# Further expert rows of a mixture-of-experts decoder layer: plain float32 products in four column tiles, bounded row gathers

## The reference

```python
A = T * TOP_K                                   # 1024 * 8 routed rows
counts = jnp.bincount(e_flat, length=N_EXPERTS)
...
def body(acc, blk):
    rows, rw, e = blk                           # a block of rows of one expert, with their weights
    xb = x_pad[rows]
    h = jax.nn.silu(xb @ w_gate[e]) * (xb @ w_up[e])    # 1024 -> 256, twice
    yb = (h @ w_down[e]) * rw[:, None]                  # 256 -> 1024
    return acc.at[rows].add(yb), None
```

## Time and profile before

| what | value |
|---|---|
| median of 3 runs | 1641.52 us (1641.01 to 1644.18) |
| the profiled execution, own time | 1632.95 us |
| its span, first to last instruction | 1631.3 us, mean granted TensorE clock 0.979 |
| PE busy | 1574.2 us (97%) |
| DVE, ACT, POOL busy | 1183.2, 1033.3, 505.7 us |
| moved by DMA | 368.63 MB |
| chain that ended last | PE 78%, DVE 7%, issue 4%, ACT 3%, DMA 3% |

### The profile page before, as it was taken

One profiled execution on the slowest core, in us unless ns is written; L12 is line 12 of the kernel. 1 busy time (PEld: TensorE's weight loads), 2 busy tenths in 40 slices (PEclk: granted clock), 3 DMA queues, 4 the chain that ended last, 5 costly groups with the idle time before them and its releaser, 6 DMA issues.

```text
span 1631.3 us, 32225 instructions
## 1 busy us (share of the span) xinstructions
PE 1574.2 (97%) x8262; PEld 1310.3 (80%) x8263; DVE 1183.2 (73%) x2038; ACT 1033.3 (63%) x1709; POOL 505.7 (31%) x495
## 2 busy tenths in 40 slices
PE   6999999999999999899999999999999999999987
PEld 6997888888887788788888888788888888888864
DVE  4215777777777788838777888767876787888856
ACT  3215666666666645427667877766776777877855
POOL 0000000000000135532544454543554455454426
PEclk9999999999999999899999999999999999999995
DMA  7223222212223524568999999999998999999987
GB/s 247 91 82 96 67 59 65 71 45 71 58 65 111 185 108 170 196 218 315 318 303 309 304 363 360 329 289 263 331 322 276 286 356 326 348 365 370 366 252 283
DMA packets 161319, 368.63 MB, mean 226 GB/s; under 512 B 53008, under 2 KB 73488, under 8 KB 161264
## 3 DMA queue, kind: packets, MB, share of 16 engines
q1 hardware_dynamic: 136272, 284.21, 49.9%
q0 software_dynamic: 24992, 83.73, 19.8%
HBM read 294.39 MB, written 65.11 MB: 220 GB/s over the span
## 4 chain that ended last, share of the span: by engine, by line
PE 78%; DVE 7%; issue 4%; ACT 3%; DMA 3%; ACTq 2%; POOL 1%; SPq 0%; DVEq 0%; POOLq 0%
PE bank_pair L1032 6%; PE bank_pair L1035 6%; PE bank_pair L1038 6%; PE q_ps L91 4%; PE out_ps L923 4%; PE q_ps L93 4%; PE q_ps L92 4%; PE k_ps L901 4%; PE out_ps L1091 4%; PE out_ps L1092 3%; PE q_ps L1022 3%; PE k_ps L1059 3%; PE k_ps L1060 2%; PE k_ps L1067 2%; DVE gu_lo L1926 2%
## 5 line engine op out<-in xcount | busy, mean ns | idle before, releaser
L1926 DVE TENSOR_TENSOR gu_lo<-raw_gu,gu_hi 128x1024 fp32r<-128x1024 f32 x260 | 306.4, 1219 | 28.7 <-ACT gu_hi L1404 28.7
L1404 ACT CAST gu_hi<-raw_gu 128x1024 fp32r<-128x1024 f32 x260 | 253.3, 1050 | 6.0 <-DMA raw_gu<-in_moe_w_up_dram 6.0
L1032 PE MATMUL bank_pair<-gu_hi,xb_hi 128*128 128x512 f32 x576 | 235.5, 409 | 5.4 <-DVE gu_lo L1926 4.2
L1035 PE MATMUL bank_pair<-gu_lo,xb_hi 128*128 128x512 f32 x576 | 229.1, 398 | 0.0
L689 POOL DMA_INDIRECT sums_scratch<-ys,sidx x63 | 119.8, 1902 | 151.7 <-DMA sums_scratch<-ys,sidx 110.6
L1926 DVE TENSOR_TENSOR dn_lo<-raw_dn,dn_hi 128x1024 fp32r<-128x1024 f32 x130 | 152.6, 1213 | 2.2 <-ACT dn_hi L1404 1.7
L1038 PE MATMUL bank_pair<-gu_hi,xb_lo 128*128 128x512 f32 x576 | 142.7, 390 | 0.0
L1032 PEld LDWEIGHTS bank_pair<-gu_hi,xb_hi 128*128 128x128 f32 x576 | 111.5, 194 | 29.5 <-issue 6.5
L1309 ACT CAST pt_hi<-k_ps 128x512 fp32r<-128x512 f32 (+1 forms) x192 | 85.9, 482 | 74.2 <-PE k_ps L901 73.4
L620 POOL IOTA e<- 128x64 f32 x1 | 0.2, 185 | 426.6 <-DVE xs L1722 426.6
L1404 ACT CAST dn_hi<-raw_dn 128x1024 fp32r<-128x1024 f32 x130 | 130.0, 1051 | 3.2 <-DMA raw_dn<-in_moe_w_down_dram 3.2
(11 more groups left out here) (306 smaller groups left out, 3971.5 us busy)
## 6 DMA issues: line engine op xcount, KB each, us to landing
raw_gu<-in_moe_w_gate_dram SPq DMA_DIRECT2D x128, 512.0 KB, 6.6
raw_gu<-in_moe_w_up_dram SPq DMA_DIRECT2D x128, 512.0 KB, 9.1
raw_dn<-in_moe_w_down_dram SPq DMA_DIRECT2D x128, 512.0 KB, 8.9
wqk<-in_fox_w_in_dram SPq DMA_DIRECT2D x66, 128.0 KB, 2.4
v_scratch<-v_out SPq DMA_DIRECT2D x32, 256.0 KB, 2.8
va<-v_scratch SPq DMA_DIRECT2D x16, 512.0 KB, 4.7
fin<-sums_scratch SPq DMA_DIRECT2D x16, 512.0 KB, 9.0
xs<-in_x_dram SPq DMA_DIRECT2D x8, 512.0 KB, 7.8
```

The lines of the kernel that those rows point to most:

```text
L1032: i = pe.matmul(o3, xb_hi[s][:, c], g_hi[:, :, c], start=c == 0, stop=False, skip_group_check=True)
L1035: pe.matmul(o3, xb_hi[s][:, c], g_lo[:, :, c], start=False, stop=False, skip_group_check=True)
L1404: a.copy(hi, raw).then_inc(S[done], 1)
L1926: dve.tensor_tensor(lo, raw, hi, ALU.subtract).then_inc(S[lo_ok], 1)
```

## The change

Further rows no longer use split operands. `xo` and `ho` hold the 32 rows as plain float32, and PE multiplies them by the raw weights. The 32 stationary columns take a quarter of PE's columns, so four products stand side by side: result rows 0 to 31, 32 to 63, 64 to 95 and 96 to 127 of the PSUM bank are four column tiles. For gate and up they are gate and up of an even chunk, and gate and up of an odd chunk; 16 matmuls of 256 columns. For down they are two chunks by two halves; 4 matmuls of 512 columns. ACT and DVE add the partial results in two pieces where there was one, and two DVE steps that made lo parts go.

Since the raw weights are now read until the further rows are done, `raw_gu` gets a third buffer (sets go to places 0, 2, 1 in turn), and the loads wait for PE: gate and up of set s for the start of `gate_up` of expert s - 3 (`started`), down of set s for the end of `down` of expert s - 3 (`downed`). Room for the third buffer comes from smaller and shared tiles: `tab` becomes 16-bit and is converted by POOL once, `gu_x` and the further results lie in free partitions of `x_rows2`. Six experts stand in a loop now, and two more before it.

The four indirect DMAs over rows get a bound of T - 1 and skip what lies above: padded slots are neither gathered nor added.

The diff, cut to its core:

```diff
-            raw_gu = [sb(f"raw_gu{i}", [P, 2, DC, FF], c=m) for i in range(2)]
+            raw_gu = [[sb(f"raw_{n}{i}", [P, DC, FF], c=m) for n in ("gate", "up")] for i in range(2)]
...
-            xo = sb("xo", [P, DC, P], F32R, c=m)
-            ho = sb("ho", [P, FC, P], F32R, c=m)
-            gu_x = sb("gu_x", [XR, 2 * FF], c=m)
-            ys = [sb(f"ys{i}", [P, D], c=m) for i in range(3)]
-            sg = sb("sg", [P, FF], c=m)
-            hh = sb("hh", [P, FF], c=m)
+            xo = sb("xo", [P, DC, XR], c=m)
+            ho = sb("ho", [P, FC, XR], c=m)
+            gu_x = xg[2][2 * XR:3 * XR, 0:2 * FF]
+            ys_x = xg[2][3 * XR:P, 0:D]
+            y_half = xg[2][2 * XR:P, BANK:D]
+            ys = [sb(f"ys{i}", [P, D], c=m) for i in range(2)]
...
+            raw_gu.append([third_gate, sb("raw_up2", [P, DC, FF], c=m)])
+            tab_in = raw_gu[2][1][:].rearrange("p c f -> p (c f)")[:, 0:TAB].bitcast(I32)
...
+        def raw_place(s):
+            return s if s < 2 else (0, 2, 1)[(s - 2) % 3]
+        def g_piece(s, k):
+            c = slice((k % 2) * 4, (k % 2) * 4 + 4)
+            return (raw_gu[raw_place(s)][k // 2][:, c], split[s % 2][0][:, k // 2, c], split[s % 2][1][:, k // 2, c])
...
+        ROUND = 6
+        ROUNDS = (E - 4) // ROUND
...
+            def next_gate_up(s, place):
+                if place > 3:
+                    sp.wait_ge(S["started"], SH + s - 2)
+                    stand(sp)
+                load_gate_up(place, *(w[ds(s - 1, 1)].rearrange("o k n -> (o k) n") for w in (w_gate, w_up)),
...
+            def next_down(s, place):
+                if place > 2:
+                    sp.wait_ge(S["downed"], SH + s - 2)
+                    stand(sp)
+                load_down(place % 2, w_down[ds(s - 1, 1)].rearrange("o k n -> (o k) n"),
...
-            next_gate_up(3, 1)
-            with sp.Fori(0, E // 2 - 2) as i:
-                for par in range(2):
-                    next_gate_up(2 * i + (par + 4), par)
-                    next_down(2 * i + (par + 3), 1 - par)
-            next_gate_up(E, 0)
-            next_down(E - 1, 1)
-            next_down(E, 0)
+            sp.dma_start(tab_in, tab_dram.rearrange("(p n) o -> p (n o)", p=P)).then_inc(S["c_loads"], 16)
+            sp.wait_ge(S["c_const"], 11)
+            next_gate_up(3, 3)
+            with sp.Fori(0, ROUNDS) as i:
+                for u in range(ROUND):
+                    next_gate_up(ROUND * i + (u + 4), u + 4)
+                    next_down(ROUND * i + (u + 3), u + 3)
+            next_gate_up(E, E)
+            next_down(E - 1, E - 1)
+            next_down(E, E)
...
-                                     in_offset=bass.IndirectOffsetOnAxis(ap=gidx[i][:, 0:1], axis=0)).then_inc(got[i], 16)
+                                     in_offset=bass.IndirectOffsetOnAxis(ap=gidx[i][:, 0:1], axis=0),
+                                     bounds_check=T - 1, oob_is_err=False).then_inc(got[i], 16)
...
-                                     in_=ys[par][:], in_offset=None, compute_op=ALU.add).then_inc(sent[par], 16)
+                                     in_=ys[par][:], in_offset=None, bounds_check=T - 1, oob_is_err=False, compute_op=ALU.add).then_inc(sent[par], 16)
...
-                    pool.wait_ge(S["c_loads"], 64)
+                    if b + 2 == SH:
+                        pool.wait_ge(S["c_loads"], 64)
+                        g.tensor_copy(tab[:], tab_in).then_inc(S["c_const"], 1)
+                        g.memset(xg[2][0:2 * XR], 0.0).then_inc(S["c_const"], 1)
+                        for i in range(2):
+                            g.memset(xg[i][:, D:ROW_W], 0.0).then_inc(S["c_const"], 1)
+                        pool.wait_ge(S["c_const"], 14)
...
-            def gate_up_further(w, x):
-                g_hi, g_lo = split[w][0:2]
-                o3 = out_ps[:, BANK:T].rearrange("p (g f) -> p g f", g=2)
-                pe.wait_ge(S["x_rows_lo_ok"], x + 1)
+            def gate_up_further(s, x):
+                raw = raw_gu[raw_place(s)]
+                pe.wait_ge(S["x_rows_ok"], x + 1)
                 pe.wait_ge(S["x_scaled"], x + 1)
-                for c in range(DC):
-                    pe.matmul(o3, xo[:, c], g_hi[:, :, c], start=c == 0, stop=False, skip_group_check=True)
-                    i = pe.matmul(o3, xo[:, c], g_lo[:, :, c], start=False, stop=c == DC - 1, skip_group_check=True)
+                for c in range(0, DC, 2):
+                    for j in range(4):
+                        i = pe.matmul(out_ps[x_tile(j), BANK:BANK + FF], xo[:, c + j // 2], raw[j % 2][:, c + j // 2], start=c == 0,
+                                      stop=c == DC - 2, skip_group_check=True)
...
-            def down_further(w, nset, x):
-                d_hi, d_lo = split[w][2:4]
-                pe.wait_ge(S["x_ht_lo_ok"], x + 1)
-                pe.wait_ge(S["d_lo_ok"], D_PIECES * nset)
-                for r in HALVES:
-                    for c in range(FC):
-                        pe.matmul(out_ps[:, r], ho[:, c], d_hi[:, c, r], start=c == 0, stop=False, skip_group_check=True)
-                        i = pe.matmul(out_ps[:, r], ho[:, c], d_lo[:, c, r], start=False, stop=c == FC - 1, skip_group_check=True)
+            def down_further(e, s, x, by_rows=True):
+                raw = raw_dn[s % 2]
+                pe.wait_ge(S["x_ht_ok"], x + 1)
+                pe.wait_ge(d_raw[s % 2], 8 * D_PIECES * (e + 1 - s % 2) + 16 * D_PIECES)
+                stand(pe)
+                for j in range(4):
+                    c, half = (j // 2, j % 2) if by_rows else (j % 2, j // 2)
+                    i = pe.matmul(out_ps[x_tile(j), BANK:T], ho[:, c], raw[:, c, HALVES[half]], start=True, stop=True, skip_group_check=True)
...
-            with pe.Fori(0, E // 2 - 1) as i:
-                for par in range(2):
-                    expert(2 * i + par, par)
-            expert(E - 2, 0)
-            expert(E - 1, 1, last=True)
+            for e in range(2):
+                expert(e, e)
+            with pe.Fori(0, ROUNDS) as i:
+                for u in range(2, ROUND + 2):
+                    expert(ROUND * i + u, u)
...
-                a.copy(gu_x[:], out_ps[XR:2 * XR, BANK:T]).then_inc(S["x_half"], 1)
+                a.copy(gu_x[:, 0:FF], out_ps[x_tile(2), BANK:BANK + FF]).then_inc(S["x_half"], 1)
+                a.copy(gu_x[:, FF:2 * FF], out_ps[x_tile(3), BANK:BANK + FF]).then_inc(S["x_up_half"], 1)
...
-                dve.tensor_tensor(gu_x[:], out_ps[0:XR, BANK:T], gu_x[:], ALU.add).then_inc(S["x_sum"], 1)
+                dve.tensor_tensor(gu_x[:, 0:FF], out_ps[x_tile(0), BANK:BANK + FF], gu_x[:, 0:FF], ALU.add).then_inc(S["x_sum"], 1)
+                dve.wait_ge(S["x_up_half"], x + 1)
+                dve.tensor_tensor(gu_x[:, FF:2 * FF], out_ps[x_tile(1), BANK:BANK + FF], gu_x[:, FF:2 * FF], ALU.add).then_inc(S["x_up_sum"], 1)
...
-                dve.tensor_tensor(ys[2][0:XR], out_ps[0:XR, :], ys[2][0:XR], ALU.add).then_inc(S["x_scaled"], 1)
+                dve.tensor_tensor(ys_x[:, BANK:D], out_ps[x_tile(1), BANK:T], ys_x[:, BANK:D], ALU.add)
+                dve.tensor_tensor(ys_x[:, 0:BANK], out_ps[x_tile(0), BANK:T], y_half[0:XR], ALU.add).then_inc(S["x_scaled"], 1)
...
```

More of the change, by code:

```diff
@@ L492, in _, with load_gate_up @@
                 weights_out(t - 1)
-            def load_gate_up(par, gate, up, left):
+            def load_gate_up(place, gate, up, left):
                 for k in range(G_PIECES):
@@ L1170, in _, with expert @@
                     logits(TT - 1)
-            def expert(e, par, last=False):
+            def expert(e, u, last=False):
+                par = u % 2
                 w = 1 - par
```

181 lines of the change are left out of this document (95 added, 86 removed).

## The result

The changed kernel takes 1780.41 us (median of 4 runs, 1774.61 to 1785.89), 1.0841 times the kernel before (95% interval 1.0794 to 1.0889). The forecast was 1581 us, and its range ended at 1618. It is slower by 139 us where 61 us less were forecast.

What follows compares the result with a forecast made beforehand. PE was taken to bound the expert stage, transfers 10% behind. PE's 726 us, 755 with partly lost smoothing, plus 11 of waits gave 766 against 827: 61 us off 1641.5, about 1581 us; range 1556 to 1618.

Steps and rivals of the forecast that it cites:

- rival (c): Six-expert loop's code no longer stays; each of ten returns waits for a fetch, 23 to 92 us, 23 taken: 1604; chance 0.15.
- PE's own time: Expert stage: each further block costs PE 2.6 us less, 78 us over 30 blocks, leaving 726 us of pure PE.
- A full drain at each of four edges: Changing PE's tiling mode might drain the engine: 1.6 us per further block, 47 us in all; 0.36 per block taken instead.
- I cost them at nothing: DVE's and ACT's changed steps stay hidden behind gate_up; without that cover, 24 us either way.
- The late loads: Later requests lose part of the smoothing between short and long bodies: stage 755 us instead of 726, plus 11 of earlier waits.
- (a): Transfers take over fully in the expert stage, no smoothing left: saving 47, with more late-load waits 40, about 1598; chance 0.18.
- (b): Skipped padded rows still take a descriptor's slot, so no transfer time is saved: floor 11.7 us per body, 1590; chance 0.08.
- Rival (d): Loads come too late for every body in the expert stage, none under 14.0 us: 55 us more, 1697; chance 0.06.
- Rival (e): Column tiles of the further products do not run side by side: 5.1 us more per block, 153 us, 1795; chance 0.02.
- Full smoothing: Best case for the expert stage: long bodies cover all transfer waits of short ones, so it takes PE's 726 us.
- the edges at nothing: Entering and leaving PE's column tiling costs nothing, instead of 0.36 us per further block; used for the range's lower end.
- The tail and POOL's start: Last expert's block in the tail gains nothing; POOL's conversion and fills, 7 us before the first gather, stay hidden.

Runs made afterwards that it cites:

- a_short: Changed kernel with loops of two experts on SP, PE, ACT and DVE; further products read fixed weights of expert 0, except the last expert's: 1627.3 us, 0.9943.
- a_lean: Changed kernel, still six experts per loop, one copy of each part and no inner loops for more than one further block: 1610.8 us, 0.9804 of the kernel before.
- s_early: a_lean_late with the load times of the kernel before, loops of two experts and fixed weights for further products: 1573.0 us, 0.9567 of the kernel before.
- a_lean_late: a_lean with PE reading its three counts after the gate and up product, not at the body's start: 1598.7 us, 0.9736 of the kernel before.
- b_va6: Kernel before with only DVE's and ACT's expert loops six experts long, PE's left at two: 1694.1 us, 1.0347.
- b_pe4: Kernel before with only PE's expert loop made four experts long: 1640.3 us, 0.9982.
- b_late: Kernel before with only the changed kernel's two waits in SP's queue, so loads are asked for later: 1666.5 us, 1.0126.
- a_compact: Changed kernel, still six experts per loop, with one copy of a body's first half and of the down product: 1691.6 us, 1.0336 of the kernel before.
- b_pe6: Kernel before with only PE's expert loop made six experts long: 1709.6 us, 1.0441.
- a_gen: Changed kernel with six experts per loop, one copy of each part, counts read late, more than one further block kept compactly: 1599.9 us, 0.9722 of the kernel before.
- ll_nobound: a_lean_late without the bounds on the four indirect transfers, so padded slots are gathered and added: 1598.0 us, 0.9720 of the kernel before.

## Why the prediction was wrong

**Where the 139 us are**, by differences of the ratios times 1641.8 us. The lines add up by construction, as each starts from the kernel at which the one before it ends, so the sum is no check. Only the third line is a single edit. The second, the fourth and the last also change the length of the loops and whether the further products read fixed weights; a_short and a_lean differ by 16 us in the shortest bodies, of the fourth line's 23:

| step | us |
|---|---|
| further products, counts covered, loads as before (s_early) | -71 |
| loads asked for later (a_lean_late against s_early) | +28 |
| counts in the open (a_lean against a_lean_late) | +11 |
| two copies and the inner loops in the code (a_short against a_lean) | +23 |
| code that does not stay (changed against a_short) | +147 |
| sum | +138 |

**The step that failed is rival (c), the loop code: its price, and then its chance.** I had the mechanism and the rule of the Trainium skill that spoke for it (Runtime: NRT & Kernel Launch, Instruction fetch mechanics), gave it 0.15, and left its cost out of the sum. I priced it as one fetch per return, 2.3 to 9.2 us, and took 23 us in all. The runs show 147 us, some 14.7 us of waits per round. PE alone fetches ten to twelve packets per round, not one; DVE and ACT fetch theirs; PE waits for them as well as for itself (57 us in b_va6), and in other bodies of the round than the one at the return. After the long wait at 1266.29 the clock costs too (0.63 us per matmul, above). The sum had no term for this: even the upper end of my own price, 92 us, is too low. That before's loops showed no fetch, told nothing of a longer one, as I wrote; b_pe4, with no loss at four experts, shows how little it told. What I had was the rule, and I went against it.

**PE's own time was nearly right.** The forecast was 12.5, 10.8 and 13.9 us for the three kinds of body with further rows. In a_lean_late they last at the least 12.49, 11.20 and 14.15 us, and the gate and up product 1.86 us where 1.79 was worked out. The shortest bodies of each kind, 63 in all, sum to 736 us; the forecast was 726. The 10 us lie in the two kinds that finish the previous expert's block. There the down product takes 1.00 us where I had 0.90, and entering it 0.18 us where I had 0.09. A full drain at each of four edges, 1.6 us per block, is ruled out: that would have left only 1.4 of the 2.6 us saved, and 2.3 were. In the changed kernel itself these times are not reached, as the next point says.

**A term put at nothing without a reason: the control code on PE between bodies.** "I cost them at nothing" was said of DVE and ACT; no run tests that by itself. For PE's control code there was no term at all. It cost nothing only because 3.64 us of matmuls stood ahead of it. Making a product shorter took that cover away: 1.34 us in the changed kernel's row, 1.6 us per block in a_short. The table has 11 us for the counts, and up to 23 for the rest of the control code.

**The late loads** came near by luck. The forecast had PE's 726 us become 755, plus 11 of old waits, 766. The stage of a_lean_late takes 779, with 10 of the 13 us from PE's own time. But the reason was wrong: what counts is when a load is asked for, not 365 GB/s. s_early moves the same bytes at 344 GB/s, and its stage takes 756 us. Rivals (a) and (b) rest on the rate and fall with it; of (b), the row does leave a packet, a small one. Rival (d) had the sign of b_late, but priced it at 55 us where b_late shows 21. Rival (e) is refuted by the four starts above.

**The lower end of the range was summed wrongly.** Full smoothing gives 726 + 11 = 737 us for the stage, 90 less than 827, and the edges at nothing 11 more: 1541 us, not 1553. It changes nothing in the outcome.

**The tail and POOL's start** did as forecast. From the end of the stage the tail takes some 50.5 us in both kernels. The conversion of the table does not show: the stage began at 759 us, and in the other runs at 755 to 766 with it and at 754 to 767 without it.

## What to carry to other kernels

Before a loop is unrolled further, compare the code of each engine's loop with what is known to stay, and count the packets of the instruction queues afterwards: here every pass of a PE loop that did not stay brought ten to twelve packets. When a product is made shorter, look at the control instructions behind it, which its length may have hidden. And test whether transfers are the limit by adding or taking bytes: here a stage at a DMA share of 1.00 took 8 MB more in the same time.

## What was not expected of the hardware

- A PE loop of 908 instructions as built (a_compact, some 2020 with weight loads and second passes) is fetched with 10 packets of 16 KB per round, as many as one of 1269 (b_pe6); one of 800 (a_gen, some 1630) is not fetched again.
- Skipping 1962 rows of some 4 KB each in the indirect queue (q0 from 19.7% of 16 engines' time in ll_nobound to 18.3% in a_lean_late) changed neither kernel's time.
- Three register loads cost PE 0.75 us per body behind the short product of a_lean, and nothing that shows behind the gate and up product of a_lean_late.
